# Moving the product-key selection's elementwise steps from VectorE to GpSimd, between its gather issues

## What is computed

```python
q = (xb @ w_q).reshape(128, 8, 2, 128)                        # per block of 128 positions
sub_s = einsum('thpc,hpnc->thpn', q, sub_keys)                # 8 heads, 2 halves, 128 keys
top_s, top_i = top_k(sub_s, 16)
cand_s = top_s[:, :, 0, :, None] + top_s[:, :, 1, None, :]    # 16 x 16 sums of key pairs
cand_i = top_i[:, :, 0, :, None] * 128 + top_i[:, :, 1, None, :]
best_s, best_j = top_k(cand_s.reshape(128, 8, 256), 16)
experts = take_along_axis(cand_i.reshape(128, 8, 256), best_j, axis=-1)
gate = softmax(best_s, axis=-1)
act = gelu(einsum('td,thkd->thk', xb, expert_u[experts]))     # a row of u and of v for each
out = einsum('thk,thkd->td', gate * act, expert_v[experts])
```

## Time and profile before

| | |
|---|---|
| median of three runs | 3476.81 us |
| profiled execution | 3469.32 us |
| its span, first to last instruction | 3467.5 us |
| first gather issued | 400.4 us |
| last gather issued | 3433.9 us |
| last group's gathers, no background | from about 2500 us |
| VectorE busy | 2137.3 us, 62% |
| TensorE busy | 2267.1 us, 65% |
| ScalarE busy | 1113.6 us, 32% |
| GpSimd busy | 1166.7 us, 34% |

### The profile page before, as it was taken

One profiled execution on the slowest core, in us unless ns is written; L12 is line 12 of the kernel. 1 busy time (PEld: TensorE's weight loads), 2 busy tenths in 40 slices (PEclk: granted clock), 3 DMA queues, 4 the chain that ended last, 5 costly groups with the idle time before them and its releaser, 6 DMA issues.

```text
span 3467.5 us, 40799 instructions
## 1 busy us (share of the span) xinstructions
PE 2267.1 (65%) x13784; PEld 1206.2 (35%) x13784; DVE 2137.3 (62%) x4890; ACT 1113.6 (32%) x3069; POOL 1166.7 (34%) x1033
## 2 busy tenths in 40 slices
PE   7788659996997765888787878577433333333333
PEld 5646534453553433333344444234211111111111
DVE  1111576657556787776777665678766566656654
ACT  2210136544331223666653332222211121122111
POOL 0000123433332323443344433333344444444443
PEclk9889779997998887888897989789666556565565
DMA  6263769999999999999999999999899999999997
GB/s 246 82 249 122 247 259 405 368 380 357 363 396 386 384 367 366 421 420 393 401 415 414 400 387 417 412 418 358 318 421 421 403 405 421 421 396 408 421 421 307
DMA packets 206838, 1265.20 MB, mean 365 GB/s; under 512 B 24779, under 2 KB 30955, under 8 KB 75556
## 3 DMA queue, kind: packets, MB, share of 16 engines
q0 software_dynamic: 147616, 1074.03, 76.5%
q1 hardware_dynamic: 59012, 188.57, 14.8%
HBM read 1247.28 MB, written 15.22 MB: 364 GB/s over the span
## 4 chain that ended last, share of the span: by engine, by line
DMA 26%; DVE 10%; PE 9%; issue 3%; ACT 2%; POOL 0%; DVEq 0%; POOLq 0%; ACTq 0%
DMA ring<-in_uv,idx 26%; PE pb L902 5%; DVE ring L1529 5%; ACT wts L1161 1%; PE pb L755 1%; DVE acc L1536 0%; DVE kidx L1442 0%; PE pb L828 0%; DVE zone L1444 0%; DVE kidx L1448 0%; DVE vals L1446 0%; ACT gl L1158 0%; PE pb L848 0%; DVE vals L1440 0%; ACT zone L1052 0%
## 5 line engine op out<-in xcount | busy, mean ns | idle before, releaser
L617 POOL DMA_INDIRECT ring<-in_uv,idx x1024 | 1163.6, 1136 | 2268.1 <-PE pb L902 1674.6
L1529 DVE CUSTOM_DVE_ANT_0 ring<-h2r,ring 128x1024 f32<-128x1024 f32 x1024 | 1233.9, 1223 | 634.2 <-DMA ring<-in_uv,idx 628.7
L902 PE MATMUL pb<-ring,wts 128*32 128x256 f32 x8192 | 745.9, 526 | 959.3 <-ACT wts L1161 959.2
L902 PEld LDWEIGHTS pb<-ring,wts 128*32 128x32 f32 x8192 | 306.6, 143 | 1370.7 <-ACT wts L1161 1109.8
L1158 ACT ACTIVATE gl<-dots 128x4 f32<-128x4 f32 x256 | 52.5, 205 | 1332.3 <-DVE dots L1529 1331.5
L944 ACT ACT_TABLE_LOAD x223 | 286.1, 1283 | 4.7 <-PEq L1676 0.7
L1161 ACT ACTIVATE wts<-gm,gl 128x32 f32<-128x32 f32 x1024 | 245.1, 310 | 8.5
L882 PE MATMUL pb<-zone,wst 128*128 128x384 f32 (+1 forms) x768 | 245.8, 476 | 1.7 <-issue 1.7
L882 PEld LDWEIGHTS pb<-zone,wst 128*128 128x128 f32 x768 | 151.8, 203 | 89.2 <-issue 23.9
L828 PE MATMUL pb<-hT,wst 128*128 128x384 f32 x512 | 175.2, 499 | 0.7 <-ACT ys L1075 0.7
L1282 DVE SCALAR_TENSOR_TENSOR zone<-pb,zone 128x384 f32<-128x384 f32 (+2 forms) x120 | 57.0, 476 | 165.1 <-ACT zone L998 163.6
(11 more groups left out here) (173 smaller groups left out, 2617.6 us busy)
## 6 DMA issues: line engine op xcount, KB each, us to landing
wst<-in_w_all SPq DMA_DIRECT2D x148, 512.0 KB, 8.5
ring<-in_w_all SPq DMA_DIRECT2D x50, 512.0 KB, 11.1
ring<-in_w_ada SPq DMA_DIRECT2D x48, 512.0 KB, 7.8
h2r<-h_scratch SPq DMA_DIRECT2D x128, 128.0 KB, 7.9
ring<-in_uv,idx POOLq DMA_INDIRECT x1024, 14.8
ys<-mod_scratch SPq DMA_DIRECT2D x9, 512.0 KB, 16.6
zone<-in_x SPq DMA_DIRECT2D x8, 512.0 KB, 4.5
hT<-in_x SPq DMA_DIRECT2D x8, 512.0 KB, 13.3
```

The source lines that it names most:

```text
L617: pool.indirect_dma_start(ring[:, n % RING, :], None, uv, bass.IndirectOffsetOnAxis(ap=idx4[:, piece % 2, col:col + 1], axis=0)).then_inc( ...
L902: m = pe.matmul(pb[32 * f:32 * f + 32, 6 + q // 2, (q % 2) * 256:(q % 2 + 1) * 256], wts[:, n % WBUFS, :], ring[:, n % RING, D + 256 * f:D ...
L1529: dve.tensor_tensor_reduce(u, h2r[:, q, :], u, 1.0, 0.0, ALU.mult, ALU.add, dots[:, n % 16:n % 16 + 1]).then_inc(dots_done, 1)
```

## The change

For pieces 1 to 31 GpSimd makes the sums of key pairs (SUMS), the cast of the key indices and the product (PICK_0, PICK_1), the sum over 16 (ADD_0, ADD_1: three halving adds and a last one, where VectorE had one reduction) and the gates' spreading (SPREAD). Piece 0 stays on VectorE. GpSimd makes the steps of slot s just before it issues gather 2s+6 (ISSUE_LEAD = 3), ahead of that gather's wait for the ring. The steps get new slots, counted from first - 22:

| | before (from first - 20) | after (from first - 22) |
|---|---|---|
| sums | 0 DVE | 0 POOL |
| best of each head | 1, 2 DVE | 2, 3 DVE |
| digits | 3, 6 DVE | 4 DVE (both) |
| comparison | 4, 7 DVE | 4, 9 DVE |
| product | 5, 8 DVE | 5, 10 POOL |
| sum over 16 | 5, 8 DVE | 6, 11 POOL |
| scores less peak, exp, gates | 9 DVE, 10 ACT, 11 DVE | 5 DVE, 6 ACT, 7 DVE |
| expert number | 9 DVE | 14 DVE |
| shuffle | 12 ACT | 15 ACT |
| index cast | 13 DVE | 16 DVE |
| spreading | 13 DVE | 17 POOL |

New semaphores tie them: `cand_ready` (VectorE waits for the sums), `decoded` (GpSimd waits for a comparison), `res_ready` (VectorE waits for a sum over 16). LEAD stands in `slots_at` too: with 22 the late query spans lie at slots 108 to 126 and at 128 and 129 (for the third group at 300 to 318, 320 and 321), and the background before them has slots up to 105 and 297, not 107 and 299. The diff, cut and with less indentation:

```diff
-LEAD = 20
+LEAD = 22
+STEP_AT = {SUMS: 0, TOP_A: 2, TOP_B: 3, DECODE: 4, PEAK: 5, EXPS: 6, GATES: 7, SAME_0: 4, PICK_0: 5, ADD_0: 6,
+           SAME_1: 9, PICK_1: 10, ADD_1: 11, EXPERTS: 14, SHUFFLE: 15, PUBLISH: 16, SPREAD: 17}
+ISSUE_LEAD = 3
 def pieces_at():
-        for k in range(14) if i else ():
-            out.setdefault(2 + k * 7 // 13 if i == 1 else first - LEAD + k, []).append((i, k))
+        for k in STEP_AT if i else ():
+            out.setdefault(2 + STEP_AT[k] * 8 // 17 if i == 1 else first - LEAD + STEP_AT[k], []).append((i, k))
 # gpsimd
+def step(piece, k):
+    if k == SUMS:
+        pool.wait_ge(tops_done, 16 * g + 2 * h1)
+        need(pool, res_ready, 2 * (piece - 1))
+        pool.tensor_tensor(c, vals[0]..., vals[1]..., ALU.add).then_inc(cand_ready, 1)
+    elif k in (PICK_0, PICK_1):
+        pool.wait_ge(decoded, 2 * (piece - 1) + p + 1)
+        link(pool.tensor_copy(fl[p][:, 0:nh], kidx[p][:, i, h0:h1]))
+        link(pool.tensor_tensor(c, c, fl[p]..., ALU.mult))
+    elif k in (ADD_0, ADD_1):
+        pool.wait_ge(sel_done, piece)
+        for half in (8, 4, 2):
+            link(pool.tensor_tensor(c[:, :, :, 0:half], c[:, :, :, 0:half], c[:, :, :, half:2 * half], ALU.add))
+        pool.tensor_tensor(res[p][:, 0:nh], c[:, :, :, 0], c[:, :, :, 1], ALU.add).then_inc(res_ready, 1)
+    elif k == SPREAD:
+        pool.wait_ge(shuffled, piece + 1)
+        if piece >= 2:
+            pool.wait_ge(w_done, last_tile(piece - 2))
+        pool.tensor_tensor(gm[:, piece % 2], mask32..., shf..., ALU.mult).then_inc(gm_done, 1)
-        pool.wait_ge(published, piece + 1)
                 for i in range(TILES):
+                    if n % 2 == 0:
+                        for s in steps.get(n // 2 - ISSUE_LEAD, ()):
+                            step(*s)
+                    if q == 0 and i == 0:
+                        pool.wait_ge(published, piece + 1)
                     need(pool, ring_free, n - RING + 1)
 # vector, tops(m)
     dve.wait_ge(s_act, 16 * g + m + 1)
+    if g:
+        dve.wait_ge(res_ready, 2 * PIECE_OF[GROUPS[g][0] - 1, m // 2])
 # vector, step(piece, k)
-    elif k in (4, 7):
+    elif k in (SAME_0, SAME_1):
+        if p:
+            need(dve, res_ready, 2 * piece - 1)
+        op = dve.tensor_tensor(c, fl[p]..., iota16..., ALU.is_equal)
+        if piece:
+            op.then_inc(decoded, 1)
...
-        link(dve.tensor_tensor(c, c, fl[p]..., ALU.mult))
-        link(dve.tensor_reduce(res[p][:, 0:nh], c, AX, ALU.add))
+    elif k == EXPERTS:
+        need(dve, res_ready, 2 * piece)
+        need(dve, shuffled, piece)
+        dve.scalar_tensor_tensor(out=sel[:, 0, ...], in0=res[0]..., scalar=float(NKEYS), in1=res[1]..., ...).then_inc(sel_done, 1)
```

More of the change, by code:

```diff
@@ L240 @@
 HALF_QUADS = 2 * 4 * 2
+SUMS, TOP_A, TOP_B, DECODE, PEAK, EXPS, GATES, SAME_0, PICK_0, ADD_0, SAME_1, PICK_1, ADD_1, EXPERTS, SHUFFLE, PUBLISH, SPREAD = range(17)
+STEP_AT = {SUMS: 0, TOP_A: 2, TOP_B: 3, DECODE: 4, PEAK: 5, EXPS: 6, GATES: 7, SAME_0: 4, PICK_0: 5, ADD_0: 6,
+           SAME_1: 9, PICK_1: 10, ADD_1: 11, EXPERTS: 14, SHUFFLE: 15, PUBLISH: 16, SPREAD: 17}
+ISSUE_LEAD = 3
 def pieces_at():
@@ L351, in build @@
         gm_done = sem("gm_done")
+        cand_ready, decoded, res_ready, pool_own = (sem(s) for s in ("cand_ready", "decoded", "res_ready", "pool_own"))
         gathered = [sem(f"gathered{i}") for i in range(RING)]
@@ L1135, in step @@
                     nh = PIECES[piece][2] - PIECES[piece][1]
-                    if k == 10:
+                    if k == EXPS:
                         tables(EXP_LN)
@@ L1139, in step @@
                         act.activation(best[:, 0:nh], best[:, 0:nh], ACT.Exp).then_inc(picked_exp, 1)
-                    elif k == 12:
+                    elif k == SHUFFLE:
                         act.wait_ge(sel_done, piece + 1)
@@ L1194, in _ @@
                     next(rest)
-                for k in (10, 12):
+                for k in (EXPS, SHUFFLE):
                     step(0, k)
@@ L1473, in step @@
                     b, h0, h1 = PIECES[piece]
-                    g = next(i for i, (lo, hi) in enumerate(GROUPS) if lo <= b < hi)
-                    i, nh = b - GROUPS[g][0], h1 - h0
+                    i, g = place_of(b)
+                    nh = h1 - h0
                     c, top = cand[:, 0:nh], best[:, 0:nh]
-                    if k == 0:
+                    if k == SUMS and not piece:
                         dve.wait_ge(tops_done, 16 * g + 2 * h1)
@@ L1514, in step @@
                         dve.wait_ge(shuffled, piece + 1)
                         dve.tensor_copy(idx4[:, piece % 2, :].rearrange("p (q n) -> p q n", q=QUARTERS), shf[:, piece % 2, 0]).then_inc(published, 1)
-                        if piece >= 2:
-                            dve.wait_ge(w_done, last_tile(piece - 2))
-                        dve.tensor_tensor(gm[:, piece % 2], mask32[:].unsqueeze(1).to_broadcast([P, QUARTERS * 8, 32]),
-                                          shf[:, piece % 2, 1].rearrange("p q n -> p (q n)").unsqueeze(2).to_broadcast([P, QUARTERS * 8, 32]),
+                    elif k == SPREAD and not piece:
+                        dve.tensor_tensor(gm[:, 0], mask32[:].unsqueeze(1).to_broadcast([P, QUARTERS * 8, 32]),
+                                          shf[:, 0, 1].rearrange("p q n -> p (q n)").unsqueeze(2).to_broadcast([P, QUARTERS * 8, 32]),
@@ L1574, in _ @@
                     next(rest)
-                for k in range(14):
+                for k in (SUMS, TOP_A, TOP_B, DECODE, SAME_0, PICK_0, ADD_0, SAME_1, PICK_1, ADD_1, PEAK, GATES, EXPERTS, PUBLISH, SPREAD):
                     step(0, k)
```

64 lines of the change are left out of this document (40 added, 24 removed).

## The result

The changed kernel takes 3482.70 us (median of 20 runs, 3474.63 to 3486.81), the kernel before 3475.14 us beside it (20 runs, 3470.20 to 3485.01): a ratio of 1.0020, 95% interval 1.0011 to 1.0028. So it is slower by 7 to 7.5 us where 12 us of gain were forecast. The time lies in the range of 3445 to 3495 us, and the loss is within the 0.3% that was called no change, but its sign is clear. The profiled execution took 3482.03 us, near its median; that of the kernel before, 3469.32 us, was at the low end of its runs. From trace to trace the difference is thus 12.7 us, and some 5 us of that are not the change's.

A forecast was written before the change was run, and what follows sets the result against it. Transfers were taken to pace 1800 of 3067 us, with 97 us the ceiling elsewhere. Terms -11.4 + 1 + 0 - 2 + 1 = -11.4, about -12, gave 3457 us profiled, 3465 on the median; range 3445 to 3495 us.

The forecast's parts named there:

- What bounds the kernel: 1360 to 2220 us and 2500 us on: paced by transfers, lighter VectorE worth nothing; elsewhere at most 97 us to win.
- What comes off VectorE: Selection work per piece: 5.0 us off VectorE, 155 us for 31 pieces; lead-ins are 1120 to 1300 and 2220 to 2400 us.
- What comes onto GpSimd: 14 instructions a piece on GpSimd: 12 us including 3 us of waiting, bounds 5.0 and 27 us, room between issues.
- Shared access: Dots on VectorE meeting GpSimd operations: held up by 2.4 us a piece, bounds nothing or all GpSimd time meeting dots.
- The schedule's shift: Stalls at 1320 and 2460 us: 7.5 us shorter each, less 1.8 us for shared access, -11.4 us in all.
- The new slots: Shuffle now after a weigh and two dots, before the index cast: +1 us in stalls and lead-ins, up to +8.
- Waits cost nothing, since 9 us of queue cover them: GpSimd steps inside a burst: two issues late by 2 to 4 us, covered by about 9 us where transfers pace.
- Slower: the shared access: Rival: GpSimd's 512-wide operations hold off dots, +22 us, 3499; decides from some 16 us a piece; slower chance 0.22.
- The gain is the shift's: Rival: moving query spans earlier alone gives the 12 us or more, same time as forecast; no chance of its own.
- Relief everywhere: Rival: lighter VectorE counts wherever transfers don't pace, dots not held up: -30 us, 3447; chance 0.11.
- Hidden or eaten up: Rival: stalls shorten, but lead-ins or 400 to 500 us take it back: 3468 to 3484 us, within 0.3%; chance 0.34.
- What the profile was to show: Signs against: dots beyond 1.22 us, 512-wide operations over 2 us, VectorE waiting for the shuffle, share under 1.01 after 2500 us.

## Point by point, why the prediction was wrong

- *What bounds the kernel.* Right for the last stage: its share stayed 1.01 and little time was won or lost there. Only half right for 1360 to 2220 us: a lighter VectorE is indeed worth nothing there, but a delay is not free. The share read 1.01 in both, while the changed kernel fell 14 us further behind from dot 272 to dot 512. The sum had 0 for this stage.
- *What comes off VectorE.* The work is right, 155 us. Its worth is the first failed step: I booked relief of 0 in 400 to 500 us, 3 in 500 to 1120, none net in the lead-ins. Alone it is worth 20 to 24 us, 6 to 8 of them before dot 64 and 7 to 8 in each lead-in. I had taken the lead-ins' share of 0.97 to leave hardly anything to win. In them VectorE is the latest engine; the runs without the work show it.
- *What comes onto GpSimd.* Right: 12 us a piece forecast, 12.6 measured. The bounds of 5.0 and 27 us held. 512-wide operations take 1.2 to 1.4 us in the mean, under the 2 us that I named. This includes time in which dots held them up; without it they take 1.06 and 1.27.
- *Shared access.* The size for the dots was right, 2.4 us a piece forecast and 64.6 / 31 = 2.1 measured. (The issue of the earlier trace rows ended 0.81 us after the dot, not 0.87.) Missing was that other operations of VectorE are met as well: the index cast alone took 23 us more.
- *The schedule's shift.* This is the step on which the forecast stood, and it failed: -11.4 us forecast, 0 measured with the lead alone. The stalls did shorten (3.7 and 6.7 us for 7.5 each). The mis-sized term is the one for the background that is packed otherwise, +1 in 500 to 1120 us and 0 in 1360 to 2220: net it measured 3.5 to 8.4 us ahead of the first stall and 5.7 to 6.4 between the two, as much as the stalls gave.
- *The new slots.* This term was all but missing: the sum had only "+1, the shuffle", with up to +8. They cost 16 to 17 us with all work on VectorE, the largest single loss. VectorE waited 22.2 us for the shuffle there, 8 times, against 4.7 us before. Moving the last four steps earlier took the wait to 6.1 us and may have won back 0.11 of the 0.47%. The rest is in the order itself, and what in it costs is open.
- *Waits cost nothing, since 9 us of queue cover them.* Not settled. The medians say 9 us, the traces nothing. The waits did make issues late by up to 5.3 us, as foreseen, which is inside the 9 us of cover taken from the median gather.
- *The rivals.* "Slower: the shared access" had the right sign for another reason: GpSimd is at 12.6 us a piece, under the 16 from which it was to decide. (By the rival's own sum, half of 11.5 pieces' excess less 12, that point lies near 18 us a piece, and 18 us gives about 0, not +10.) "The gain is the shift's" is out, the shift gains nothing. "Relief everywhere" was right that relief pays off the paced stages, 20 to 24 us where it booked 18 over the forecast, but sharing and order came with it. "Hidden or eaten up" is the nearest in time and in kind.
- *What the profile was to show.* Dots beyond 1.22 us, and VectorE waiting for the shuffle (24.9 us), were named as signs against the forecast, and both came. The second turned out to cost nothing that the run with the earlier shuffle could show. The third sign, a share under 1.01 after 2500 us, did not come.

Open stay: what in the second half of the new order costs VectorE so much; what the waits cost by themselves; why waits and sharing cost 28 us at the old slots and 10 at the new; and whether fewer hand-overs could keep part of the 24 us. None of the versions run here that do all the work beats the kernel before beyond its interval.

## What to carry to other kernels

To price an offload, leave the work out first: one run gives the most that it can bring, here 24 us. Run the new order with the work left where it is: it gives what the order costs, here 17 us. A busy share of 1.01 does not say that a delay in that stage is free; its GB/s and the progress of the work have to be read beside it. A difference of medians that the traces can't place is not yet a cause. And a stall that gets shorter is no gain until the stretch before it has been looked at with the same care.

## What was not expected of the hardware

- A small VectorE operation can be held until a GpSimd operation ends: the 32-wide index cast took up to 2.28 us beside a spread of 1.92 us, against 0.18 us alone. It was held up 12 times in 32, 11 of them by the spread, which waits for the same shuffle.
- The means of GpSimd's operations hide what they cost alone, since a dot holds them up. The last add of 32 elements a partition took 0.48 us in the mean but 0.24 in the median, the product 1.41 and 1.27. Without such hold-ups float32 operations took 0.24 us for 32 elements, 0.29 for 64, 0.73 for 256, 1.06 (sum) and 1.27 (product) for 512 and 1.91 for 1024. VectorE took 0.69 us for 512.
- An issue that followed the product on GpSimd began 0.84 us after it (30.9 us in 37 cases), against 0.30 us between two issues and 0.16 us after a spread (2606.65 to 2606.81). After the last add, which like the spread isn't linked, it is 0.53 us (2577.04 to 2577.56). So the gap depends on which waits stand between the two, not on the operation's length alone.
